# One hybrid attention layer on one core: x stored feature-major, row sums on TensorE in column groups, probabilities scaled from a bank, the gate row in two parts

## The reference, cut to what matters

```python
mod = silu(c) @ ada_w + ada_b                        # 1024 -> 3072
shift, scale, gate = split(mod, 3)
h = rmsnorm(x, pre_norm_w) * (1 + scale) + shift
proj = h @ w_in                                      # 1024 -> 4104
mq, mk, mv, mg, dq, dk, dv, dz, db, da = split(proj) # 8 widths of 512, two of 4
o_moba = softmax_attention(rope(mq), rope(mk), mv) * silu(mg)     # 8 heads of 64, causal
dq, dk, dv = silu(causal_conv4([dq, dk, dv]))
o_dn = rmsnorm(gated_delta_rule(dq, dk, dv, g(da), sigmoid(db)))  # 4 heads of 128, chunks of 64
y = [o_moba, o_dn * silu(dz)] @ w_out
out = x + gate * rmsnorm(y, post_norm_w)
```

## Time and profile before

| | |
|---|---|
| median of the runs | 200.72 us |
| the profiled execution, its own time | 201.38 us |
| its span | 199.2 us |
| PE busy | 185.7 us (93%) |
| DVE busy | 138.4 us (69%) |
| ACT busy | 104.1 us (52%) |
| POOL busy | 83.4 us (42%) |
| moved by DMA | 38.43 MB |

### The profile page before, as it was taken

How to read it: one execution, slowest core, us unless ns; L and a number is a source line. 1 busy time by engine, 2 the same in 40 slices (tenths; PEclk the granted TensorE clock), 3 DMA queues, 4 the chain that set the end, 5 groups by cost and what they waited for, 6 DMA issues and landing times.

```text
span 199.2 us, 4716 instructions
## 1 busy us (share of the span) xinstructions
PE 185.7 (93%) x1898; PEld 170.3 (86%) x1898; DVE 138.4 (69%) x326; ACT 104.1 (52%) x201; POOL 83.4 (42%) x46
## 2 busy tenths in 40 slices
PE   7999779999999989999999999997999999899970
PEld 6897769999999989988989999896999987588850
DVE  0638989463079988979878646746989399837364
ACT  2835445636398869396553226385234548337230
POOL 2037709795969616928065003974000220504000
PEclk9988999999999999999999999999999999999998
DMA  5999999999106530197308400062029357910022
GB/s 211 394 403 404 409 396 407 400 406 408 42 0 207 175 147 0 44 396 305 105 3 273 151 3 3 3 212 106 3 74 412 151 205 223 359 59 0 3 107 105
DMA packets 11527, 38.43 MB, mean 193 GB/s; under 512 B 1393, under 2 KB 1521, under 8 KB 10994
## 3 DMA queue, kind: packets, MB, share of 16 engines
q1 hardware_dynamic: 11362, 37.61, 50.6%
q10 hardware_dynamic: 144, 0.52, 0.7%
HBM read 37.08 MB, written 1.05 MB: 191 GB/s over the span
## 4 chain that ended last, share of the span: by engine, by line
PE 51%; DVE 28%; DMA 8%; ACT 6%; issue 3%; POOL 1%; DVEq 0%; SPq 0%; ACTq 0%; POOLq 0%
PE bank L1337 11%; PE bank L1338 10%; PE bank L1339 10%; DVE cv L951 7%; DVE accg L1139 5%; DMA raw<-in_w_out 4%; PE bank L1348 4%; DVE bank L926 3%; DMA outb<-in_post_norm_w 3%; PE bank L1547 3%; PE bank L1558 3%; PE bank L1535 2%; DVE pr L1114 2%; ACT whi L544 1%; DVE ssq L1003 1%
## 5 line engine op out<-in xcount | busy, mean ns | idle before, releaser
L471 POOL TENSOR_TENSOR wlo<-raw,whi 128x1024 fp32r<-128x1024 f32 (+1 forms) x25 | 57.4, 2317 | 66.7 <-ACT whi L544 66.7
L1337 PE MATMUL bank<-hhi,whi 128*128 128x256 f32 x224 | 65.3, 292 | 3.0 <-DVE hlo L895 2.1
L1338 PE MATMUL bank<-hhi,wlo 128*128 128x256 f32 x224 | 63.6, 284 | 0.0
L1339 PE MATMUL bank<-hlo,whi 128*128 128x256 f32 x224 | 63.5, 283 | 0.0
L1337 PEld LDWEIGHTS bank<-hhi,whi 128*128 128x128 f32 x224 | 43.1, 193 | 5.2 <-DVE hlo L895 2.9
L1338 PEld LDWEIGHTS bank<-hhi,wlo 128*128 128x128 f32 x224 | 43.2, 193 | 0.0
L1339 PEld LDWEIGHTS bank<-hlo,whi 128*128 128x128 f32 x224 | 43.1, 193 | 0.0
L544 ACT ACTIVATE whi<-raw 128x1024 fp32r<-128x1024 f32 (+1 forms) x33 | 33.0, 1026 | 10.6 <-PE bank L1339 7.5
L951 DVE SCALAR_TENSOR_TENSOR cv<-bank,convh,cv 128x255 f32<-128x255 f32 (+2 forms) x36 | 17.0, 481 | 8.6 <-ACT cv L608 7.6
L926 DVE SCALAR_TENSOR_TENSOR bank<-ada,sml,bank 128x512 f32<-128x512 f32 (+1 forms) x24 | 16.5, 687 | 0.7
L485 POOL TENSOR_TENSOR rot<-rot,cst 128x512 f32<-128x512 f32 x4 | 4.4, 1091 | 22.3 <-DVE rot L1081 20.4
(11 more groups left out here) (203 smaller groups left out, 359.0 us busy)
## 6 DMA issues: line engine op xcount, KB each, us to landing
raw<-in_w_rest SPq DMA_DIRECT2D x20, 512.0 KB, 5.1
ada<-in_ada SPq DMA_DIRECT2D x12, 512.0 KB, 8.7
ada<-in_gate_w SPq DMA_DIRECT2D x4, 1024.0 KB, 8.3
raw<-in_w_out SPq DMA_DIRECT2D x8, 512.0 KB, 6.2
ada<-in_ada SPq DMA_DIRECT2D x8, 256.0 KB, 6.1
raw<-in_w_qkv SPq DMA_DIRECT2D x5, 384.0 KB, 7.7
qkvs<-in_w_qkv SPq DMA_DIRECT2D x4, 384.0 KB, 9.2
cv<-in_w_qkv SPq DMA_DIRECT2D x4, 384.0 KB, 13.6
```

What stands on the lines that cost most here:

```text
L471: pool.tensor_tensor(split_u(wlo, n), raw_u(n), split_u(whi, n).bitcast(F32), ALU.subtract).then_inc(lo_done, 1)
L1337: pe.matmul(out, a[0][ia], b[0][ib], start=start, stop=False, skip_group_check=skip)
L1338: pe.matmul(out, a[1][ia], b[0][ib], start=False, stop=False, skip_group_check=skip)
L1339: return pe.matmul(out, a[0][ia], b[1][ib], start=False, stop=stop, skip_group_check=skip)
```

## The change

Five things are changed together.

- x comes feature-major (`x_turned`), in two loads of the same sizes and on the same queues as before. ACT squares blocks 0 to 3, DVE blocks 4 to 7. TensorE sums the squares over the features: eight products with 32 columns of ones as weights, which write four groups of 32 partitions of one bank (`rows_of_four`), then two small ones turn the sums into columns (`x_sums`). After root and reciprocal two products spread the factors over a bank (`x_spread`), and DVE multiplies x by it, piece by piece (`x_scale`). The 16 transposes and the copies out of the banks are gone.
- Pieces 0 and 1 of `silu(c) @ ada_w` are made by TensorE alone in the same four groups (`mod_rows`), copied by ACT and summed by `mod`. DVE adds up pieces 2, 3 and 4 only. Piece 0 of h goes to `hhi` straight from x.
- `normalise(m)` puts the reciprocals into a bank and scales with two `tensor_tensor` instructions over both heads, which read the factor from there; the last instruction of `maxima(m)` is a `scalar_tensor_tensor` with ones.
- The gate row is split into hi and lo parts before its sum over the partitions (`gate_hi` on ACT, `gate_lo` on DVE), and summed by two fp32r products.
- The lists of calls of all engines, the order of the transfers and `DVE_LO` (eight units to six) are written anew.

```diff
+            def x_square(b):                                      # ACT; DVE has b = 2, 3
+                act.wait_ge(x_loaded[0], 16)
+                act.activation(xsq[:, 2 * b:2 * b + 2, :], xT[:, 2 * b:2 * b + 2, :], ACT.Square).then_inc(xsq_done, 1)
+            def rows_copy(p):
+                act.wait_ge(rows_made, p + 1)
...
+                act.activation(acc[:, p % 2, 0:256], bank[7][:, 0:256], ACT.Copy).then_inc(rows_copied, 1)
+            def x_scale(p):                                       # DVE
+                k0, n = PIECES[p]
+                dve.wait_ge(rs_ready, 1)
+                a = xT[:, k0:k0 + n, :]
+                dve.tensor_tensor(a, a, bank[5][:, S:].unsqueeze(1).to_broadcast([P, n, S]), ALU.mult).then_inc(xn_done, 1)
...
+            def rows_of_four(b, k, stationary, moving):           # TensorE
+                g = slice(32 * (k % 4), 32 * (k % 4) + 32)
+                return pe.matmul(bank[b][g, 0:256], stationary, moving, start=(k < 4), stop=(k >= 4), skip_group_check=True)
+            def x_rows(k):
...
+                ins = rows_of_four(5, k, ones[:, 0:32], xsq[:, k, :])
+            def mod_rows(p, k):
...
+                pe.wait_ge(*ada_ready(p, k))
+                ins = rows_of_four(7, k, sml[:, 24 + k:25 + k].to_broadcast([P, 32]), ada_piece(p)[:, k, :])
...
             def normalise(m):
                 dve.wait_ge(p_done, 4 * (m + 1))
-                link(dve.reciprocal(stat[:, 72 + 4 * m:76 + 4 * m], stat[:, 32 + 4 * m:36 + 4 * m]))
-                for e in range(2):
-                    for qt in range(NT):
-                        o, w, i = qt * P, (qt + 1) * P, 72 + 4 * m + 2 * e + qt
-                        ins = dve.tensor_scalar(pr[:, e, o:o + w], pr[:, e, o:o + w], stat[:, i:i + 1], None, ALU.mult)
+                inv = bank[ATT[1]][:, 384:388]
+                link(dve.reciprocal(inv, stat[:, 32 + 4 * m:36 + 4 * m]))
+                inv = inv.rearrange("p (e t) -> p e t", e=2)
+                for qt in range(NT):
+                    o, w = qt * P, (qt + 1) * P
+                    ins = dve.tensor_tensor(pr[:, :, o:o + w], pr[:, :, o:o + w], inv[:, :, qt:qt + 1].to_broadcast([P, 2, w]), ALU.mult)
                 ins.then_inc(pn_done, 1)
...
+            def gate_lo(i):
+                dve.wait_ge(gate_hi_done, i + 1)
+                dve.tensor_tensor(g_lo, accg[:, i * 512:(i + 1) * 512], g_hi.bitcast(F32), ALU.subtract).then_inc(gate_split, 1)
...
             def gate_sum(i):
-                pe.wait_ge(gate_acc, NK * (i + 1))
+                pe.wait_ge(gate_split, i + 1)
...
-                pe.matmul(bank[6][:, :], ones[:, :], accg[:, i * 512:(i + 1) * 512], start=True, stop=True).then_inc(gate_ready, 1)
+                pe.matmul(bank[6][:, :], g_ones, g_hi, start=True, stop=False)
+                pe.matmul(bank[6][:, :], g_ones, g_lo, start=False, stop=True).then_inc(gate_ready, 1)
...
-        DVE_LO = (21, 34, 35, 37, 38, 41, 42, 43)
+        DVE_LO = (29, 31, 33, 40, 41, 42)
```

More of the change, by code:

```diff
@@ L754, in _ @@
             hi(9)
-            ba_hi()
             hi(10)
@@ L1263, in _ @@
             mask_z(0, 0)
-            maxima(1)
-            v_tokens(1)
             mask_z(0, 1)
-            rope(2)
-            normalise(1)
             mask_z(1, 0)
@@ L1271, in _ @@
             merge(1, 0)
+            merge(1, 1)
+            maxima(1)
             q_decayed(0)
-            merge(1, 1)
             mask_z(2, 0)
@@ new lines, in x_rows, with x_sums @@
+            def x_rows(k):
+                pe.wait_ge(ones_set, 1)
+                if k < 4:
+                    pe.wait_ge(xsq_done, k // 2 + 1)
+                else:
+                    pe.wait_ge(xsq1_done, (k - 4) // 2 + 1)
+                ins = rows_of_four(5, k, ones[:, 0:32], xsq[:, k, :])
+                if k == NK - 1:
+                    ins.then_inc(xrows_ready, 1)
+            def x_sums():
+                pe.wait_ge(dve_init, 1)
+                pe.wait_ge(xrows_copied, 1)
+                for t in range(NT):
+                    ins = pe.matmul(bank[5][:, S + t:S + t + 1], acc[:, 1, t * P:(t + 1) * P], epsc[:, 2:3], start=True, stop=True)
+                ins.then_inc(xsum_ready, 1)
@@ new lines, in x_spread @@
+            def x_spread():
+                pe.wait_ge(front_loaded, 16)
+                pe.wait_ge(xrstd_done, 1)
+                for t in range(NT):
+                    ins = pe.matmul(bank[5][:, S + t * P:S + (t + 1) * P], sml[:, 20 + t:21 + t].to_broadcast([P, P]), ident, start=True, stop=True)
+                ins.then_inc(rs_ready, 1)
+            def mod_rows(p, k):
+                if p == 0:
+                    pe.wait_ge(sc_done, 1)
+                if p == 1:
+                    pe.wait_ge(mod_read, 1)
+                pe.wait_ge(*ada_ready(p, k))
+                ins = rows_of_four(7, k, sml[:, 24 + k:25 + k].to_broadcast([P, 32]), ada_piece(p)[:, k, :])
+                if k == NK - 1:
+                    ins.then_inc(rows_made, 1)
@@ L1714, in y_products @@
                     ins.then_inc(unit_done, 1)
-            busy(1, 3)
-            busy(3, 8)
-            mod_direct(2)
-            mod_direct(3)
-            busy(2, 1)
-            mod_direct(4)
-            mod(0)
-            mod_direct(5)
-            busy(0, 1)
-            mod_direct(6)
-            mod_direct(7)
-            x_turn(0)
-            x_turn(1)
-            x_turn(2)
-            x_turn(3)
-            qkv_products(0)
+            busy(1, 9)
+            x_rows(0)
+            x_rows(1)
+            x_rows(4)
+            x_rows(5)
+            x_rows(2)
+            x_rows(3)
+            x_rows(6)
+            x_rows(7)
+            mod_rows(0, 0)
+            mod_rows(0, 1)
+            mod_rows(0, 2)
+            mod_rows(0, 3)
+            x_sums()
+            mod_rows(0, 4)
+            mod_rows(0, 5)
+            mod_rows(0, 6)
+            mod_rows(0, 7)
+            x_spread()
+            mod(0)
+            busy(1, 3)
+            qkv_products(0)
+            mod_rows(1, 3)
+            mod_rows(1, 1)
+            mod_rows(1, 5)
+            mod_rows(1, 0)
+            mod_rows(1, 4)
+            mod_rows(1, 2)
+            mod_rows(1, 6)
+            mod_rows(1, 7)
             mod(1)
@@ L1803, in _ @@
             t_turn(5, 0)
-            z_products(4, 1)
+            pv(1)
+            half(12)
             z_products(5, 0)
-            p_turn(1)
-            half(12)
-            pv(1)
             x_products(4, 1)
             x_products(5, 0)
+            z_products(5, 1)
+            t_turn(5, 1)
             scores(2)
```

417 lines of the change are left out of this document (209 added, 208 removed).

## The result

The changed kernel takes 205.01 us (median of 4 runs, 204.64 to 205.15), the kernel before 200.63 on the same chip: ratio 1.0202, interval 1.0173 to 1.0231. It is slower, by 1.7 to 2.3%; 197.2 was predicted. The profiled execution took 204.91 us with a span of 203.1.

The account below looks back on a forecast made before the run. Opening bound by DVE and data, then by PE with a few holes. 1.7 + 1.3 + 1.0 − 0.5 = 3.5 us off the profiled 201.38 gives 197.9, as a median 197.2; range 194.9 to 199.9.

Parts of the forecast that it names:

- the opening: Up to the last q, k, v block: earlier products, PE's lead growing to some 4 us by 31 us, data the floor.
- The third, slower one: Rival: DVE's gate sums wait for POOL products; 206 us, or 201.8 to 203 with half of them; chance 0.12.
- The first product: Opening: first product with weights at 13.1 us, 2.6 us earlier than before.
- The clock at the start: First unit: PE's clock at 0.50 for 3 to 4 us, leaving a lead of about 1.5 us.
- nine dummies instead of 22: Start of PE's work: fewer dummies precede it, which speaks against the change, since activity releases the slow clock.
- case 2: Rival: opening's lead lost, sums one by one at 1.2 GHz, 0.43 us each; 198.6, up to 200 us; chance 0.22.
- The last block: Last q, k, v block: starts 2.0 us earlier (bounds 0.8 and 2.6); unit 14 lands at 47.0, lo(15) ends at 51.5.
- a sign of being wrong: Opening: the prediction is wrong if POOL's lo(15) isn't bound by the landing of unit 14.
- The middle: From the last block to half(8), DVE's and ACT's chain: lead at half(8) 1.7 us (bounds 0.5 and 3).
- The 0.3 us that I took off: Between the last block and half(8): the lead was put at 2.0 us, then 1.7.
- Probabilities and end: After half(8): 1.3 us from scaling probabilities, 1.0 from the earlier load_last for the second gate sum, minus 0.5 for new waits.
- the bound of 1.4: Scaling of the probabilities: upper bound of its 1.3 us gain (bounds 0 and 1.4).

Follow-up runs that it names:

- run 9: Run 1 with only one of the twelve dummy products ahead of the first unit left: 200.36 us, ratio 0.9946 to the kernel before.
- run 8: Run 1 with row sums and pieces 0 and 1 made by products with 128 weight columns, no column groups: 202.61 us, ratio 1.0074 to the kernel before.
- run 6: Run 1 with DVE's modulate(2) ahead of all sums of piece 3 and h_lo(2) behind only two of them: 197.83 us, ratio 0.9834 to the kernel before.
- run 1: The changed kernel with one ACT call, ba_hi, moved back behind hi(9): 198.67 us, ratio 0.990 to the kernel before.
- run 10: The kernel before with only the new normalise and end of maxima: 199.22 us, ratio 0.9907 to the kernel before.
- run 11: Run 1 with the old normalise and end of maxima: median 203.13 us, ratio 1.0011 to the kernel before.

## Why the prediction was wrong

**The step that failed** is in the opening: "PE's own lead could grow from 1.5 to some 4 us by 31 us", with only the data as a floor. I had added up what DVE no longer does and followed ACT up to the first `h_hi`, but had not gone down ACT's list call by call behind it. `ba_hi` had moved up, past `modulated(3)` and `modulated(2)`. That is a moved wait: ahead of a load of which the landing (31.04) could be read in the trace before, with `modulated(2)`, `h_hi(2)`, DVE's `h_lo(2)` and `qkv(4)` queued behind it. 31.0 plus the 2.7 us of these steps is 33.7, where `qkv(4)` had started at 30.3 before and was to start at least 2 us earlier: over 5 us late, from rows of before. None of the rivals had it. The third, slower one named a blocked DVE instruction at the gate sums; those took 0.75 us each, with POOL idle. That the measured 205.0 lies between this rival's 201.8 and 206 is chance.

**The first product**: 13.73 for 13.1. The order of steps was right; the row sums end at 9.1 and ACT's root starts at 10.24, with `hi(0)` only behind it (10.42), so the copy of piece 0 comes at 11.17 and the steps behind it follow 0.5 us later than I had them.

**The clock at the start**: wrong. I expected 0.50 for 3 to 4 us at the first unit; it was at 1.00 from 4.3 us on, and at the first unit even with one dummy left (run 9). The remark that nine dummies instead of 22 speak against the change sets products against passes: before, 22 passes are eleven products. In the changed kernel only the 6.6 us wait let the clock fall. For the same reason the price in case 2, 0.43 us for a product alone at the slow clock, is off: in run 8 eight passes of four such products take 1.97 us, 0.43 us a product, at full clock.

**The last block**: with the moved call taken back, 0.7 us earlier (53.11) where 2.0 was forecast, and 1.4 in run 6. Unit 14 landed at 47.6 (forecast 47.0) and POOL ended `lo(15)` at 52.1 to 52.25 (forecast 51.5), so the floor was 0.6 off; in run 1 it wasn't the floor but DVE's order that decided, sums of piece 3 ahead of `modulate(2)` and `h_lo(2)`. In the changed kernel POOL ended it at 58.3, since PE's delay held back the buffers: there `lo(15)` wasn't bound by the landing of unit 14, which the prediction had named as a sign of being wrong.

**The middle**: the lead at the last block arrives at `half(8)` nearly as it is, 0.75 in run 1 (89.42 to 90.17); what run 8 is late at the last block against run 1 (3.8 us), it is at `half(8)` too. The 0.3 us that I took off did not show, and neither did a gain.

**Probabilities and end**: the sum of 1.8 was met in the profiled executions, 90.17 to 199.2 being 109.0 us before and 95.89 to 203.1 107.2 now. The one before lies 0.66 above its median, so this is good luck in part. Its division was not. The new scaling alone (run 10) shortens this part to 106.8 us (89.91 to 196.7), 2.2 less: it takes away PE's wait for `pr` and, as everything on DVE comes earlier, the wait at the second gate sum too. The prediction had put that wait down to the load of `post_norm_w` rightly, but counted it to the new order of the gate sums: in run 10 the load is issued at 163.1 instead of 164.8 and lands after 5.9 us instead of 6.7. What remains of the change in this part costs about 0.4 us by these spans, less than single executions can tell. And the bound of 1.4 held for the old order only: in the new one the old scaling costs 2.2 us by the ratio and up to 4.5 by the median (run 11), so the new form is what makes that order pay.

**The whole**: with the one call back in its place the kernel takes 198.67 us, the change's gain is 2.0 us (1.3 to 2.7) instead of 3.5. Of the 1.5 us short, 1.0 is the opening's (0.75 at `half(8)` for 1.7); the rest is within the interval. Run 6, at 197.83, is 3.3 us (2.8 to 3.9) faster than before.

## What to carry to other kernels

When a list of calls is written anew, go down each engine's list call by call, the cheap ones too: for each call that moved, put the landing or the end that it waits for, from the trace before, beside the new time at which its turn comes, and then name all that is queued behind it. A copy of 0.26 us that waits costs what the wait costs, not what the copy does. And if TensorE idles for several microseconds because of it, reckon with a slower clock afterwards: here 1.6 us on top of 4.8 for a wait of 6.6 us, while a wait of 2 us cost the clock in some executions only.

## What was unexpected of the hardware

- Four fp32 products in four column groups took 0.64 us from first start to last end, the same four with 128 columns 1.97 us; an fp32 product of 256 columns is two passes of 0.215 us at full clock, while an fp32r one took 0.12.
- After the same wait of some 2 us before `qkv(4)` the granted clock fell to 1.2 GHz for 3.4 us in the profiled executions of runs 9 and 11 and stayed at 2.4 GHz in that of run 1, with the same list of products ahead of it in runs 1 and 11.
- Where the trace has no record of the clock, the windows print 1.00. With one dummy the first record begins at 9.34, and the passes ahead of it take 0.63 us instead of 0.38.
- The old scaling beside POOL did not cost a fixed price: the same program took between 200.46 and 205.62 us from one execution to the next. In the one trace of it, an instruction that starts while a POOL product runs takes 2.2 to 2.4 us instead of 0.3, and the clock falls after the wait; how the scatter divides between the two is not shown.
